# First stage by output tile of the modulation, and the recurrent stage's taps at other places

## What is computed

```python
mod = c @ w_ada[layer] + b_ada[layer]
sh_a, sc_a, gt_a, sh_m, sc_m, gt_m = jnp.split(mod, 6, axis=-1)
h = modulate(rmsnorm(x, g_mix[layer]), sh_a, sc_a)
z = h @ w_in[layer]
...
u = glu_in[..., :D_CONV] * jax.nn.sigmoid(glu_in[..., D_CONV:])
u = lax.conv_general_dilated(u, conv_w[:, None, :], ..., feature_group_count=D_CONV) + conv_b
```

## Time and profile before

| | us |
|---|---|
| median of 3 runs | 2215.86 |
| lowest, highest | 2214.8, 2217.65 |
| profiled execution, its own time | 2215.59 |
| its span in the trace | 2213.8 |
| TensorE busy | 2081.9 |
| VectorE busy | 1154.8 |

### The profile page before, as it was taken

One profiled execution on the slowest core, in us unless ns is written; L12 is line 12 of the kernel. 1 busy time (PEld: TensorE's weight loads), 2 busy tenths in 40 slices (PEclk: granted clock), 3 DMA queues, 4 the chain that ended last, 5 costly groups with the idle time before them and its releaser, 6 DMA issues. The chain is left out here.

```text
span 2213.8 us, 35978 instructions
## 1 busy us (share of the span) xinstructions
PE 2081.9 (94%) x14896; PEld 1645.4 (74%) x14896; DVE 1154.8 (52%) x1803; ACT 785.2 (35%) x1292; POOL 731.0 (33%) x347
## 2 busy tenths in 40 slices
PE   5898889999899999989999999999999998999997
PEld 5785566788688888767767777776777787888886
DVE  6426776333552432746677778667723457524322
ACT  2335656223332332442334333333334434323221
POOL 0321020434344444352332233233223343444442
PEclk9979999999899999989999999999999999999998
DMA  7541011543133333331111111111123332333331
GB/s 263 181 136 45 30 47 38 178 133 102 60 101 97 95 95 97 101 107 32 40 47 37 37 40 47 35 40 44 44 66 121 115 97 75 96 97 103 96 95 67
DMA packets 52465, 186.88 MB, mean 84 GB/s; under 512 B 5840, under 2 KB 6992, under 8 KB 51920
## 3 DMA queue, kind: packets, MB, share of 16 engines
q1 hardware_dynamic: 48528, 174.49, 25.3%
q10 hardware_dynamic: 3776, 10.09, 1.3%
HBM read 178.27 MB, written 6.29 MB: 83 GB/s over the span
## 5 line engine op out<-in xcount | busy, mean ns | idle before, releaser
L682 POOL TENSOR_TENSOR wlo<-raw,whi 128x1024 fp32r<-128x1024 f32 x266 | 643.7, 2420 | 1314.5 <-ACT whi L1298 1314.5
L765 PE MATMUL psum<-ah,whi 128*128 128x512 f32 x1288 | 540.7, 420 | 28.8 <-POOL wlo L682 16.9
L766 PE MATMUL psum<-ah,whi 128*128 128x512 f32 x1288 | 514.2, 399 | 0.0
L767 PE MATMUL psum<-ah,wlo 128*128 128x512 f32 x1288 | 512.9, 398 | 0.0
L1298 ACT ACTIVATE whi<-raw 128x1024 fp32r<-128x1024 f32 x266 | 280.1, 1053 | 358.0 <-PE psum L767 292.6
L765 PEld LDWEIGHTS psum<-ah,whi 128*128 128x128 f32 x1288 | 248.3, 193 | 102.5 <-POOL wlo L682 27.3
L767 PEld LDWEIGHTS psum<-ah,wlo 128*128 128x128 f32 x1288 | 248.6, 193 | 54.9
L766 PEld LDWEIGHTS psum<-ah,whi 128*128 128x128 f32 x1288 | 249.3, 194 | 43.4 <-issue 0.2
L2008 DVE SCALAR_TENSOR_TENSOR x<-upad,vec,x 128x512 f32<-128x512 f32 x240 | 210.7, 878 | 5.1
L765 PE MATMUL psum<-hidden,whi 128*128 128x512 f32 x536 | 209.8, 392 | 0.1
L766 PE MATMUL psum<-hidden,whi 128*128 128x512 f32 x536 | 209.5, 391 | 0.0
(11 more groups left out here) (340 smaller groups left out, 2850.5 us busy)
## 6 DMA issues: line engine op xcount, KB each, us to landing
raw<-in_w SPq DMA_DIRECT2D x322, 512.0 KB, 3.6
x<-in_x SPq DMA_DIRECT2D x1, 2048.0 KB, 8.1
x_kept<-x ACTq DMA_DIRECT2D x1, 2048.0 KB, 9.5
ao_kept<-ao ACTq DMA_DIRECT2D x8, 256.0 KB, 2.2
aof<-ao_kept ACTq DMA_DIRECT2D x1, 2048.0 KB, 10.8
x<-x_kept ACTq DMA_DIRECT2D x1, 2048.0 KB, 9.2
out<-x SPq DMA_DIRECT2D x8, 256.0 KB, 2.5
lwt<-in_lw ACTq DMA_DIRECT2D x8, 128.0 KB, 2.1
```

The lines of the kernel that those rows point to most:

```text
L682: pool.tensor_tensor(wlo[:, s % NHL, :], raw_of(SPLITS[s]), whi[:, s % NHL, :].bitcast(F32), ALU.subtract).then_inc(lo_done, 1)
L765: pe.matmul(dst, wh, h_, start=first, stop=False)
L766: pe.matmul(dst, wh, l_, start=False, stop=False)
L767: return pe.matmul(dst, wl, h_, start=False, stop=last)
```

## The change

**Modulation by output tile.** The sixteen blocks ("ada", 0 or 1, k) become sixteen blocks ("mod", m, half): four k at a time, the 128 shift and the 128 scale columns of output tile m only. VectorE folds 256 columns at a time (`take_mod`, eight for a tile), TensorE sums them by two matmuls (`sum_mod`, into the eighth bank), and VectorE writes the tile's two columns (`mod_tile`). x times the reciprocal root is made by GpSimd (into space of qT, ksd, kwd); ScalarE applies scale and shift and makes the high part, VectorE the low part between the folds of the next tile. TensorE does seven products at once (`AHEAD`: z11, z4, z12, z5, z13, z14, z15), k-outer: at tile m, `begun(m)` = m + 2 of them, at most seven, have begun, and a new one catches up on the tiles before. The first 23 blocks have eleven places (four of `raw`, seven of `raw_first`), the seven high and low weights have places of their own, and the compression's blocks have six (`raw_ck`), which may be filled once the seventh product is done. x is loaded in four pieces, the column vectors in two. The squares of x are summed on VectorE and reduced once. What was FRONT without the seven products comes behind in a new order. ada(2) to ada(5) each move to a later place: ada(2) behind the first attention, ada(3) among the gates, ada(4) behind the first output product, and ada(5) beside the first MLP, with a block and a fold beside each of its first eight products.

**Taps.** Their number is the same; the counts in the slots come from a list, two taps stand at the start of a tile, two behind gnv and three behind pt. The reciprocal of kkss becomes a step kkinv behind the taps of its slot.

```diff
+AHEAD = [("z", 11), ("z", 4), ("z", 12), ("z", 5), ("z", 13), ("z", 14), ("z", 15)]
+FRONT = [("z", 10), ("bkv", 0), ("z", 7), ("bkv", 1), ("ck", 0, 0), ("ss", "cq"), ("ck", 0, 1), ("z", 9), ("root", "cq"), ("ck", 0, 2), ("ck", 0, 3),
+         ("z", 6), ("norm", "cq"), ("ck", 1, 0), ("ck", 1, 1), ("ck", 1, 2), ("z", 8), ("kc",), ("ck", 1, 3), ("gt",), ("vt", 0), ("vt", 1),
+         ("ss", "ckv"), ("z", 0), ("root", "ckv"), ("vc",), ("norm", "ckv")]
...
+def begun(m):
+
+    return min(m + 2, len(AHEAD))
...
-    out = [("raw", ("ada", s, k)) for s in range(2) for k in range(KT)]
+    out = []
+    for m in range(KT):
+        out += [("raw", ("mod", m, half)) for half in range(2)]
+        out += [("split", f) for f in AHEAD[begun(m - 1) if m else 0:begun(m)]]
...
+            wait_emptied(pool, ("rb", "mix"))
+            for m in range(KT):
+                pool.tensor_tensor(spread_x[m], x[:, m, :], sq_sum[:, 1, :], ALU.mult).then_inc(x_scaled, 1)
+                weights_ahead(min(m, len(AHEAD) - 1))
...
+            def sum_mod(m):
+
+                pe.wait_ge(mod_taken, KT * m + KT)
+                for i in range(2):
+                    mm = pe.matmul(psum[:, OBANK, 2 * m + i:2 * m + i + 1], mod_sum[m % 2][:, i * P:i * P + P], ones[:, 0:1], start=True, stop=True)
+                mm.then_inc(mod_summed, 1)
...
+            for m in range(KT):
+                had = begun(m - 1) if m else begun(m)
+                for e in range(had):
+                    ahead(e, m)
+                    if e == 1 and m + 1 < KT:
+                        sum_mod(m + 1)
+                for e in range(had, begun(m)):
+                    for k in range(m + 1):
+                        ahead(e, k)
...
+            for m in range(KT):
+                n = EVENT["mix", m]
+                act.wait_ge(x_scaled, m + 1)
+                act.wait_ge(mod_ready, 2 * m + 2)
...
+                act.activation(tmp[:, n % NTMP, :], spread_x[m], ACT.Identity, bias=mod[:, m:m + 1], scale=modg[:, m:m + 1]).then_inc(pre_split, 1)
+                high(("mix", m), ah[:, 0, m, :])
+                weights_ahead(begun(m + 1) - 1)
...
+            for m in range(KT):
+                if m == 0:
+                    mod_tile(m)
+                for k in range(KT if m + 1 < KT else 0):
+                    take_mod(m + 1, k)
+                    if m and k == 1:
+                        mod_tile(m)
+                    if k == 4:
+                        low(("mix", m), ah[:, 0, m, :], ah[:, 1, m, :])
+                if m == KT - 1:
+                    mod_tile(m)
+                    low(("mix", m), ah[:, 0, m, :], ah[:, 1, m, :])
...
+TAPS = (0, 2, 2, 2, 2, 0, 2, 2, 2, 0, 2, 2, 1, 2, 0, 3)
...
-        out += [("tok", j, 0), ("mb", j, 0), ("tok", j, 1), ("mb", j, 1), ("iy0", j, 0), ("iy0", j, 1)]
+        out += [("conv", j, 2), ("tok", j, 0), ("mb", j, 0), ("tok", j, 1), ("mb", j, 1), ("iy0", j, 0), ("iy0", j, 1)]
...
-        out += [("akv", j, 0), ("akv", j, 1), ("inv", j, 1, 0), ("opv", j)]
+        out += [("conv", j, 2), ("akv", j, 0), ("akv", j, 1), ("inv", j, 1, 0), ("opv", j)]
...
-        out += [("opa", j)] + last[:1] + [("pt", j, 0), ("pt", j, 1)] + last[1:2] + [("qq", j, 0), ("qq", j, 1)]
+        out += [("opa", j)] + last[:1] + [("pt", j, 0), ("pt", j, 1), ("conv", j, 3)] + last[1:2] + [("qq", j, 0), ("qq", j, 1)]
...
+                elif kind == "kkinv":
                     dve.wait_ge(kkroot_done, j + 1)
                     dve.reciprocal(nrt[:, :], nrt[:, :]).then_inc(nrm_ready, 1)
...
+                            if (n, c) == (1, 0):
+                                ada_take(5, m)
```

More of the change, by code:

```diff
@@ L102, in weight_blocks @@
     for m in range(16):
-        out += [("split", ("gate", m)), ("raw", ("ada", 4 + m // KT, m % KT))]
+        out += [("split", ("gate", m)), ("raw", ("ada", 3 + m // KT, m % KT))]
     out += [("split", ("nm", m)) for m in range(KT)]
@@ L121, in mlp_blocks @@
 def mlp_blocks(n):
-    return [("split", (f"fc{half}", n, c, m)) for half, c in mlp_order() for m in range(KT)]
+    out = []
+    for half, c in mlp_order():
+        for m in range(KT):
+            out += [("split", (f"fc{half}", n, c, m))] + ([("raw", ("ada", 5, m))] if (n, half, c) == (1, 1, 0) else [])
+    return out
 def parts(what, n):
@@ L157, in rwkv_order, with slot @@
         last = parts(("glu", j + 1, 0), KT) if j + 1 < KT else []
-        def slot(taps):
+        taps = list(TAPS)
+        def slot():
             got = [ahead.pop(0)] if ahead else []
-            while ahead and ahead[0][0] != "part":
+            while ahead and ahead[0][0] not in ("part", "kkinv"):
                 got.append(ahead.pop(0))
-            return got + [("conv", j, taps)]
-        out += [("tok", j, 0), ("mb", j, 0), ("tok", j, 1), ("mb", j, 1), ("iy0", j, 0), ("iy0", j, 1)]
+            got.append(("conv", j, taps.pop(0)))
+            return got + ([ahead.pop(0)] if ahead and ahead[0][0] == "kkinv" else [])
+        out += [("conv", j, 2), ("tok", j, 0), ("mb", j, 0), ("tok", j, 1), ("mb", j, 1), ("iy0", j, 0), ("iy0", j, 1)]
         if j:
@@ L204, with raw_slots @@
 BLOCK_AT = {what: b for b, (_, what) in enumerate(BLOCKS)}
+def raw_slots():
+    slot, turn, before = [], [], []
+    latest, rest, cks = {}, 0, 0
+    for b, (_, what) in enumerate(BLOCKS):
+        if b < 2 * KT + len(AHEAD):
+            n = b % (NRAW + RAW_FIRST)
+        elif what[0] == "ck":
+            n, cks = NRAW + RAW_FIRST + cks % RAW_CK, cks + 1
+        else:
+            n, rest = (rest + 1) % NRAW, rest + 1
+        before.append(latest.get(n))
+        turn.append(0 if before[-1] is None else turn[before[-1]] + 1)
+        slot.append(n)
+        latest[n] = b
+    return slot, turn, before
+RAW_SLOT, RAW_TURN, RAW_BEFORE = raw_slots()
 SPLIT_AT = {}
@@ new lines, in mod_tile @@
+            def mod_tile(m):
+                dve.wait_ge(mod_summed, m + 1)
+                both = psum[:, OBANK, 2 * m:2 * m + 2]
+                dve.tensor_tensor(mod[:, m:m + 1], both[:, 0:1], vcol("b_ada", m), ALU.add).then_inc(mod_ready, 1)
+                dve.scalar_tensor_tensor(modg[:, m:m + 1], both[:, 1:2], mod[:, KT + m:KT + m + 1], vcol("g_mix", m), ALU.add,
+                                         ALU.mult).then_inc(mod_ready, 1)
+            for k in range(1, KT):
+                add_square("mix", k)
@@ L1765, in _ @@
             dve.wait_ge(vec_loaded, 16)
+            step(dve.tensor_scalar(mod[:, KT:2 * KT], vcol("b_ada", KT, KT), 1.0, None, ALU.add))
             for k in range(KT):
-                ada_take(0, k)
-            mean_square("mix", D)
-            for k in range(KT):
-                ada_take(1, k)
                 if k == 2:
+                    mean_square("mix", D)
+                if k == 4:
                     inverse_root("mix")
-            ada_done(0)
-            ada_done(1)
-            wait_emptied(dve, ("ada", 1))
@@ L1782, in _ @@
                 if kind == "z":
-                    ada_take(*ada_beside(f)[1:])
-                elif kind == "ada":
-                    ada_done(f[1])
+                    for what in ada_beside(f):
+                        ada_take(*what[1:])
                 elif kind == "bkv":
@@ L2280, in block_of @@
     w_in = w["w_in"]
+    if kind == "mod":
+        m, k0 = what[1], 4 * what[2]
+        parts_of = [w["w_ada"][k * P:k * P + P, s * D + m * P:s * D + m * P + P] for k in range(k0, k0 + 4) for s in range(2)]
+        return np.concatenate(parts_of, 1)
     if kind == "ada":
```

230 lines of the change are left out of this document (141 added, 89 removed).

## The result

The changed kernel takes 2197.8 us (median of five runs, 2192.9 to 2206.3) beside 2215.9 us (2214.5 to 2218.7) of the kernel before: ratio 0.993, interval 0.9908 to 0.9952. It is faster by 18 us where the forecast was 38, and 1.8 us above the range's upper end. The five runs lie 13 us apart and those of before 4; but in a later comparison 17 runs of the kernel before lay 11 us apart, so the spread alone shows little.

A forecast was written before the change was run, and what follows sets the result against it. TensorE, busy 94% of the span, was taken as the bound, so gains come from its standing still or half clock. Recurrent stage -16.8, first stage -22.6, ada(5) +1.8 make -37.6: 2215.9 to about 2178 us, range 2158 to 2196.

The forecast's parts named there:

- the recurrent part: Recurrent stage: moved taps fit VectorE's gaps, TensorE's waits for ip and iy go, 2.4 us a tile, -16.8 us in all.
- D: Recurrent stage: TensorE's waits reappear at another instruction, 3 us gained instead of 17, 2192 us; chance 0.12.
- C: Modulation loop: TensorE stays cold and never recovers, loop ends at 93 us instead of 79.5, 2192 us; chance 0.14.
- E: Whole front: TensorE at half clock, attention starts later than 187 us, 2240 us, slower than before; chance 0.03.
- B: First stage: VectorE-GpSimd exclusion hardly costs, seven products end at 64 us, 15.5 earlier, 2163 us; chance 0.20.
- the waits for ip and iy: Recurrent stage: TensorE's waits on VectorE, 1.7 and 0.7 us a tile, were to go.
- ada(5) cost what was said: First MLP: ada(5) at full clock adds 1.8 us; no new TensorE wait in the MLP.
- Step 4: First stage: VectorE's 40 us and about 25 of GpSimd's add up; seven products end at about 79.5 us.
- Step 5: From seventh product to attention: 56 us work, 6 waits, 8 half clock, 70 in all; attention near 149.5 us, -22.6.
- the sign named for the exclusion: Modulation loop: mean of VectorE's 256-column folds well over 0.5 us, over 0.8; a mean of 0.5 would show B.

The follow-up runs named there:

- experiment 6: Changed kernel, three taps between pt and qq kept, plus six unread 128x128 matmuls on TensorE ahead of each tile's second state step: 2188.6 us, ratio 0.9881.
- experiment 1: Changed kernel with no taps between pt and qq, its three taps there moved to other places: 2178.6 us, ratio 0.9845 to the kernel before.
- experiment 3: Changed recurrent stage alone, on the first stage of the kernel before: 2221.2 us, ratio 1.0034 to the kernel before.
- experiment 2: Changed first stage alone, with taps and inverse root placed as in the kernel before: 2196.6 us, ratio 0.992 to the kernel before.
- 4: Changed kernel with two taps between pt and qq in place of three: 2186.8 us; with one tap there: 2179.1 us.
- experiment 7: Kernel with no taps between pt and qq, GpSimd filling the first seven weights' low halves with zeros instead of subtracting: 2162.0 us, ratio 0.9759.

## Why the prediction missed

**The step that failed** stands in the recurrent part: "three at 2.3 us into the 2.76 us gap", and behind it "each fits, with 0.3 to 0.5 us to spare". The gap and its length were right, and 2.3 us is what three taps take where VectorE is alone (2.32 in the trace after). What I had not looked up is who else works in that gap. In the trace of before GpSimd's split and arow lie there too, from 1308.73 us to 1312.22, and su starts at 1311.91:

```profile
1308.73 2.37 POOL L682 TENSOR_TENSOR wlo<-raw,whi 128x1024 fp32r<-128x1024 f32 x1 [4.70 <-ACT whi L1298]
1311.05 1.17 POOL L732 TENSOR_TENSOR arow<-rkv,ewall 128x512 f32<-128x512 f32 x1
```

And the earlier trace rows had given the rule with which I priced the first stage: such an operation waits until GpSimd's ends. By it the first tap ends just behind the split and the second just behind arow: the 4.97 us are 2.04 of the split, 2.1 of taps and about 0.8 of arow's 1.63. The same rule was used in one stage and left out in the other.

**What it cost.** Without these three taps the kernel takes 2175.4 to 2179.1 us in three comparisons, about 2178; with them 2197.8. Of these 20 us the pause is about 11 (experiment 6 against 1: 2188.6 to 2178; 7 tiles of 1.42 us are 9.9, and the unread matmuls cost 1.1 in the eighth, which has no pause to fill) and the half clock behind it about 9 (2197.8 to 2188.6; 15 in the profiled execution, which was the slowest). The forecast's sum had no term for the half clock.

**The rivals.** D was the right kind: the waits came back at another instruction. But it named the iy of level 5, had them give back 14 us (3 gained instead of 17), and took the clock as unmoved; they gave back more than all, and the half is slower than before by experiment 3. C, cold TensorE in the modulation loop, didn't come: 0.83 was the lowest ten microseconds of the loop. The same loop in experiments 2 and 4 had 0.62 from 40 to 50 us, and attention began at 153.8 to 154.1 us there, about where the other traces have it, so half clock in the middle tiles costs nothing that shows. E needed attention to start behind 187 us; it starts at 153.5. B isn't there, since the exclusion is. Experiment 7 takes the splits away, though not GpSimd's products of x, and lands at 2162.0 us where B said 2163; that is luck in part, for B had the seven products end at 64 us and there they end at 75.5.

**What was right.** The other places for taps fit: the waits for ip and iy went, and a tile is 75.18 us without the three taps (forecast 75.4). ada(5) cost what was said and no MLP wait came. The first stage with it: 17.6 us in experiment 2, forecast 20.8. Put together, the parts that held give the 2178 that experiment 1 measures. That agreement has some luck in it, since the first stage was 3 to 4 us short and a whole kernel's time is known to some 4 us.

**The first stage's terms.** Step 4 said 79.5 us for the end of the seven products; it is 88.5 (behind the last low half at 82.28 the last of their triples starts at 87.85). Step 5 said 70 us from there to the attention; it is 65. The loop in the changed kernel, by the group of the folds and by VectorE's timeline:

```profile
L1892 DVE SCALAR_TENSOR_TENSOR mod_sums<-raw_first,vec,mod_sums 128x256 f32<-128x256 f32 x34 | 28.9, 850 | 1.2
```

```profile
27.36 2.82 DVE L1835 SCALAR_TENSOR_TENSOR ah<-tmp,ah 128x512 fp32r<-128x512 f32 x1
...
66.35 0.69 DVE L1835 SCALAR_TENSOR_TENSOR ah<-tmp,ah 128x512 fp32r<-128x512 f32 x1
...
71.74 0.16 DVE L1899 TENSOR_TENSOR mod<-psum,vec 128x1 f32<-128x1 f32 x1 [2.48 <-PE psum L1037]
...
80.41 0.16 DVE L1899 TENSOR_TENSOR mod<-psum,vec 128x1 f32<-128x1 f32 x1 [4.66 <-PE psum L1037]
...
82.28 0.69 DVE L1835 SCALAR_TENSOR_TENSOR ah<-tmp,ah 128x512 fp32r<-128x512 f32 x1 [1.60 <-ACT ah L1442]
```

The fold's mean is over 0.8 us (0.81 with the 22 folds of the other places), the sign named for the exclusion. Take the two waits of 2.48 and 4.66 us off 82.28 and the last low half would stand at 75.1, where the forecast had 74. By this working the exclusion was sized right and the waits, which the sum put at nothing, are the missing term; no run takes the waits alone away. They are for the small matmuls that sum the modulation (L1037), which stand in TensorE's queue behind triples of earlier tiles, and from 64 us on TensorE works without a pause. The forecast let VectorE set the end, with seven triples behind it; but TensorE comes to the sixth tile with a backlog (from 66.4 to 88.5 us it does some 32 triples of 0.68 us, where the last three tiles have 26), and VectorE waits for it.

The Trainium skill, on the page SBUF — State Buffer, section "SBUF: two separate sides", has the port pair of VectorE and GpSimd as a lock held for a whole instruction, and against a VectorE operation with two SBUF inputs only by a GpSimd operation that reads SBUF. The runs agree on both, but for some 0.2 us of a tap that passed beside the split (alone it takes 0.75 us, and it ended 0.54 us behind the split): 2.59 us for one tap beside a split, and folds of 0.57 us beside memsets of 0.95 us where they took 0.85 beside splits. On its page TensorE: Matmul & The Clock Gate, section "A second HAM failure mode: psum-queue depth-cycling", the Trainium skill tells of a kernel whose short idle times between groups of matmuls made the clock go back and forth; experiment 6 agrees, in that the clock stays at 1.00 once the one pause of 1.45 us a tile is filled.

**What stays open.** Why the clock falls behind one pause and not behind the next of the same length: in the changed kernel one full tile in six escaped, with two taps four in six, and with the old first stage (experiment 3) none. Nor is it the pause's length alone, or small matmuls behind it. The kernel before has pauses of up to 1.10 us ahead of 32 matmuls of 64x64, and its clock is 1.00 through the whole tile:

```profile
1295.02 1.15 PE L1173 MATMUL psum<-iy,ip 64*64 64x64 f32 x32 [1.10 <-DVE ip L2145]
...
1242.20:1320.00 77.80, 74.72 (x999) 56.26 (x1000) 56.52 (x98) 27.36 (x44) 22.04 (x13) 1.00 0.13 41
```

This is probably also why the halves don't add up: 17.6 us gained and 7.0 lost make 10.6, and the whole gained 18.

## What to carry to other kernels

An idle gap of VectorE is worth its length only if GpSimd is idle in it too: before work with two SBUF inputs is moved there, read GpSimd's timeline over the same microseconds and count one operation per GpSimd operation. A new wait of TensorE costs its own length and, as here ahead of the state steps, perhaps as much again in half clock; whether it does can't be told from its length, so look at the granted clock behind each one. For the same reason a gap should be filled to leave the consumer on time in every tile rather than nearly. And a rule taken from one row of a trace should be put to every stage that the change touches before the sum is made.

## What the runs showed of the hardware

- Six unread matmuls in a pause of 1.45 us made the kernel 9 us faster (2188.6 against 2197.8) and its tiles equal to 0.04 us.
- A pause of 0.7 us ahead of the second state step was enough to bring the lower clock in two tiles of six, while pauses of up to 1.10 us ahead of ip left it at 1.00 in the kernel before.
- A tap of 0.7 us took 2.59 us beside a split that began 0.32 us ahead of it. GpSimd's arow took 1.63 us beside taps and 1.17 to 1.19 us without: it is held up in its turn.
